# A four-layer transformer kernel: the forget-gate chain in two parts about the compressed keys, compression weights halved between ScalarE and GpSimd, and four other edits in order

## The reference

```python
def hybrid_layer(x, norm_g, w_in, ...):
    h = rmsnorm(x, norm_g)
    proj = h @ w_in
    ...
    o_nsa = nsa_mixer(nsa_q, nsa_kv, nsa_g, cmp_pos, cmp_w1, cmp_b1, cmp_w2, cmp_b2)
    o_pool = pool_mixer(pool_in, pool_w, pool_scale)
    c_x, c_b, c_c = jnp.split(conv_in, 3, axis=-1)
    o_conv = conv_mixer(c_x, c_b, c_c, conv_w)
    f_q, f_k, f_v = jnp.split(fox_qkv, 3, axis=-1)
    o_fox = fox_mixer(f_q, f_k, f_v, fox_f, fox_f_bias)
    ...
def nsa_compress(k, pos_emb, w1, b1, w2, b2):     # the compressed keys and values
    blocks = k[:, idx] + pos_emb                  # 32 tokens each, stride 16
    flat = blocks.reshape(B, nc, NSA_CMP_LEN * hd)
    return jax.nn.silu(flat @ w1 + b1) @ w2 + b2
def fox_mixer(q, k, v, f_logit, f_bias):          # the forget gate
    logf = jax.nn.log_sigmoid(f_logit + f_bias)
    c = jnp.cumsum(logf, axis=1)
    ...
        s = s + jnp.transpose(c_blk, (0, 2, 1))[..., None] - c_keys[:, :, None, :]
def pool_mixer(u, pool_w, pool_scale):            # means over 2, 4, 8, 16 tokens, less u
    ...
    mixed = jnp.einsum('btgc,gcd->btgd', pooled, pool_w).reshape(B, T, C)
    return mixed * pool_scale
```

## Time and profile before

| | |
|---|---|
| median of 3 runs | 2528.85 us (2526.66 to 2528.97) |
| profiled execution, device time | 2527.82 us |
| its span, first to last instruction | 2526.0 us |
| TensorE busy | 2424.8 us (96%) |
| GpSimd busy | 1898.6 us (75%) |
| VectorE busy | 1149.5 us (46%) |
| ScalarE busy | 690.9 us (27%) |
| mean granted TensorE clock | 0.987 |

### The profile page before, as it was taken

One profiled execution on the slowest core, in us unless ns is written; L12 is line 12 of the kernel. 1 busy time (PEld: TensorE's weight loads), 2 busy tenths in 40 slices (PEclk: granted clock), 3 DMA queues, 4 the chain that ended last, 5 costly groups with the idle time before them and its releaser, 6 DMA issues.

```text
span 2526.0 us, 32296 instructions
## 1 busy us (share of the span) xinstructions
PE 2424.8 (96%) x11118; PEld 1871.2 (74%) x11118; DVE 1149.5 (46%) x1587; ACT 690.9 (27%) x1242; POOL 1898.6 (75%) x1553
## 2 busy tenths in 40 slices
PE   7989989999999999899999999999999999999998
PEld 6755768888877843678888777767888877678886
DVE  6576563330261477643322474555322645553323
ACT  2166233330021157233320133144010231450101
POOL 8703578888877753698888799735999998359995
PEclk9999999999999999999999999999999999999999
DMA  4201122222222210122222232201222222112222
GB/s 175 84 9 43 51 75 100 98 93 100 92 75 100 85 41 1 67 100 91 100 97 95 75 113 100 84 34 59 100 97 94 92 100 85 41 53 99 99 99 84
DMA packets 57547, 207.11 MB, mean 82 GB/s; under 512 B 6512, under 2 KB 6896, under 8 KB 57200
## 3 DMA queue, kind: packets, MB, share of 16 engines
q1 hardware_dynamic: 55872, 199.87, 22.2%
q10 hardware_dynamic: 1584, 5.96, 0.6%
HBM read 203.71 MB, written 2.10 MB: 81 GB/s over the span
## 4 chain that ended last, share of the span: by engine, by line
PE 76%; DVE 10%; POOL 7%; issue 4%; ACT 2%; DMA 1%; POOLq 0%; DVEq 0%; ACTq 0%; SPq 0%
PE bank L719 21%; PE bank L721 20%; PE bank L720 20%; POOL w_hi L2526 4%; PE bank L813 4%; PE bank L768 3%; POOL w_lo L2529 3%; PE bank L841 2%; PE bank L867 2%; PE bank L888 1%; DVE branch_lo L1842 1%; DVE moving_lo L1842 1%; DVE x L2168 1%; DVE work L1882 1%; PE bank L906 1%
## 5 line engine op out<-in xcount | busy, mean ns | idle before, releaser
L2526 POOL TENSOR_TENSOR w_hi<-ring,unit 128x512 fp32r<-128x512 f32 x750 | 846.4, 1129 | 497.3 <-PE bank L721 357.0
L2529 POOL TENSOR_TENSOR w_lo<-ring,w_hi 128x512 fp32r<-128x512 f32 x750 | 1010.6, 1347 | 58.7
L719 PE MATMUL bank<-moving_hi,w_hi 128*128 128x512 f32 x1962 | 776.3, 396 | 26.8 <-DVE moving_lo L2137 12.3
L721 PE MATMUL bank<-moving_hi,w_lo 128*128 128x512 f32 x1962 | 768.8, 392 | 0.0
L720 PE MATMUL bank<-moving_lo,w_hi 128*128 128x512 f32 x1962 | 768.7, 392 | 0.0
L719 PEld LDWEIGHTS bank<-moving_hi,w_hi 128*128 128x128 f32 x1962 | 371.5, 189 | 116.9 <-issue 25.7
L720 PEld LDWEIGHTS bank<-moving_lo,w_hi 128*128 128x128 f32 x1962 | 371.4, 189 | 78.8 <-issue 1.9
L721 PEld LDWEIGHTS bank<-moving_hi,w_lo 128*128 128x128 f32 x1962 | 371.1, 189 | 78.4
L2473 DVE TENSOR_TENSOR region<-region,bank 128x512 f32<-128x512 f32 x64 | 39.7, 682 | 278.4 <-PE bank L721 278.4
L719 PE MATMUL bank<-hid_hi,w_hi 128*128 (+1 forms) x352 | 137.7, 391 | 0.0
L1780 ACT ACTIVATE region<-bank 128x512 f32<-128x512 f32 x64 | 38.1, 598 | 363.4 <-PE bank L721 363.4
(11 more groups left out here) (299 smaller groups left out, 3441.1 us busy)
## 6 DMA issues: line engine op xcount, KB each, us to landing
ring<-in_weights SPq DMA_DIRECT2D x375, 512.0 KB, 3.2
x<-in_x_t ACTq DMA_DIRECT2D x4, 512.0 KB, 8.4
out<-region SPq DMA_DIRECT2D x8, 256.0 KB, 2.2
region<-in_tables ACTq DMA_DIRECT2D x1, 1312.0 KB, 9.3
region<-in_tables ACTq DMA_DIRECT2D x1, 1024.0 KB, 5.7
region<-in_p_t ACTq DMA_DIRECT2D x2, 512.0 KB, 4.9
region<-in_tables SPq DMA_DIRECT2D x1, 320.0 KB, 10.4
small_w<-in_small_w ACTq DMA_DIRECT2D x1, 320.0 KB, 5.9
```

The costliest lines, as they stand in the source:

```text
L719: pe.matmul(bank, lhs[0], rhs[0], start=start, stop=False, skip_group_check=True)
L721: return pe.matmul(bank, lhs[1], rhs[0], start=False, stop=stop, skip_group_check=True)
L2526: pool.tensor_tensor(w_parts[0][:, s, at], ring[:, s, at], unit[:, 0:1].broadcast_to([P, BLK // 2]), ALU.mult).then_inc(split_hi, 1)
L2529: pool.tensor_tensor(w_parts[1][:, s, at], ring[:, s, at], w_parts[0][:, s, at].bitcast(F32), ALU.subtract).then_inc(split_ready, 1)
```

## The change

Six edits, none of which changes a result or the number of matmuls:

1. **Start**: ScalarE's four copies of the `vA` banks stand ahead of the sines.
2. **Join**: for the layer norm ahead of a feed-forward, VectorE joins `x = hi + lo` and makes the lower part of `p` behind the feed-forward's loop instead of ahead of it. The residual and ScalarE's scaling of `x` wait for a new semaphore `x_joined`.
3. **Compression weights**: ScalarE makes the upper part of the `w1` blocks (`upper_w1`: two instructions a block, when the block is loaded and the half of the ring is free), at four places of its `project_second`. GpSimd makes the lower part alone and waits for the new semaphore `w1_upper` before it (`split_w1`). These blocks stand outside GpSimd's loops, so its one long loop becomes three.
4. **Forget gate**: the first four instructions of the chain stand ahead of `vc_bd`, the last six behind `cmp_p`.
5. **Pool products**: they are issued in the middle of block conv5 and go to banks 4 to 7. The banks of conv4 and conv5 become 0 and 2.
6. **Heads**: the scores of turn 0 wait for `cb1` and `cu0`, those of turn 1 for `cu1` too, and only the transposes behind them for `pm3`.

```diff
+CONV_BANK = (0, 1, 2, 3, 0, 2)
...
                 for u, i in turns[:AHEAD]:
+                    if second and i == 1:
+                        second()
                     scores(u, i, q, k, extra, causal)
...
+                if opened:
+                    opened()
...
-                for t, before in enumerate(("fv0", "fv1", "fv2", "fv3", "cx0", "cx1")):
+                def pool_products():
+                    prepared_at("pooled")
+                    for g in range(4):
...
+                        pe.matmul(psum[4 + g][rows, :], small_w[rows, at:at + HD], mix[rows, 2 + g // 2, :], start=True,
+                                  stop=True).then_inc(spread, 1)
+
+                for t, before in enumerate(("fv0", "fv1", "fv2", "fv3", "cx0", "cb0")):
                     stored_at(before)
-                    project(("conv", layer, t), psum[t % 4][:], rhs)
+                    project(("conv", layer, t), psum[CONV_BANK[t]][:], rhs, halfway=pool_products if t == 5 else None)
...
-                pe.wait_ge(stored, T["stored"][("pm3", layer)])
+                pe.wait_ge(stored, T["stored"][("cb1", layer)])
+                pe.wait_ge(prepared, T["prepared"][("cu0", layer)])
...
@@ scalar
+                values(range(4), ("vA", 3), lambda i: v_ab[:, i, :], lambda i: psum[i])
+
                 act.wait_ge(setup_dve, SETUP["rest"])
                 act.activation(sin_a, rest[:, 0, :], ACT.Sin)
...
                 raw(("nq1", layer), nq[:, 1, :], psum[1][:], HD ** -0.5)
+                upper_w1(layer, 0)
...
                     store(fqk[:, t, :], psum[2 - 2 * t][:], scale=HD ** -0.5)
+                    upper_w1(layer, 1 + t)
...
                     store(fqk[:, 2 + t, :], psum[1 + t][:])
+                    if t == 0:
+                        upper_w1(layer, 3)
...
+            def upper_w1(layer, i):
+                n = AT[("w1", layer, i)]
+                act.wait_ge(full[n % RING], 16 * (n // RING) + 16)
+                for h, spent in enumerate((half_done, block_done)):
+                    at = slice(h * BLK // 2, (h + 1) * BLK // 2)
+                    act.wait_ge(spent, n - RING + 1)
+                    act.activation(w_parts[0][:, n % RING, at], ring[:, n % RING, at], ACT.Copy).then_inc(w1_upper, 1)
@@ vector
-                dve.wait_ge(parts_ready, T["parts"][("ln", i, KD - 1)])
+                if i % 2:
+                    dve.wait_ge(parts_ready, T["parts"][("ln", i, KD - 1)])
+                    join_parts()
...
-                lower(("p", layer), both(p_parts, np.s_[:, :, :]), p_in_t)
                 with dve.Fori(0, KF // 2) as it:
...
+                join_parts().then_inc(x_joined, 1)
+                lower(("p", layer), both(p_parts, np.s_[:, :, :]), p_in_t)
...
@@ gpsimd
+            def split_w1(n):
+                key, s = BLOCKS[n], n % RING
+                for h in range(2):
+                    at = slice(h * BLK // 2, (h + 1) * BLK // 2)
+                    pool.wait_ge(w1_upper, 8 * key[1] + 2 * key[2] + h + 1)
+                    pool.nop().then_inc(split_hi, 1)
+                    pool.tensor_tensor(w_parts[1][:, s, at], ring[:, s, at], w_parts[0][:, s, at].bitcast(F32),
+                                       ALU.subtract).then_inc(split_ready, 1)
...
+            for layer in range(DEPTH):
+                for i in range(4):
+                    n = AT[("w1", layer, i)]
+                    split_up_to(at, n)
+                    split_w1(n)
+                    at = n + 1
             split_up_to(at, len(BLOCKS))
```

## The result

The changed kernel takes **2499.49 us** (median of 4 runs, 2498.30 to 2500.55), the kernel before beside it 2528.91 (2526.66 to 2530.61). The ratio is 0.9884, 95% interval 0.9872 to 0.9896: 29.4 us saved. The forecast was 2493 and 35.9 us saved. The measured time lies in the range, but at its slower half, so 6.5 us of the forecast gain are missing and have to be found.

What follows compares the result with a forecast made beforehand. TensorE was busy 96% of the span, leaving only its idle time and the pauses' clock cost to gain. Terms 4.3 + 4.8 + 9.8 + 13.0 + 4.0 = 35.9 us gave 2491.9, as a median 2493; range 2486 to 2504.

Steps and rivals of the forecast that it cites:

- Start: Start of the program: ScalarE's copies first let TensorE go on at 35.0 instead of 37.95; 4.3 us with the clock's price.
- Join: Behind the feed-forward loop: the third tile's wait and three short stalls on GpSimd go, 2 x 2.4 us.
- Compression weights: From w1(1) to pool0: ScalarE's upper parts remove TensorE's waits on GpSimd and the clock behind them, 2 x 4.9 us.
- Forget gate: At the transposes of `cmp_p`: the 4.12 us wait and 2.4 us of low clock behind it go, 2 x 6.5 us.
- Pool products: Last convolution matmul to the heads' first maximum: products and stores move into conv5; with the heads, 2 x 2.0 us.
- Heads: Opening of the heads: first maximum 1.2 us after conv5's end, in one term with the pool products, 2 x 2.0 us.
- with slack: At w1(0), where ScalarE comes late: GpSimd ends the block about 0.6 us later than before, with slack.
- The handovers: Rival at the compression weights: handovers between engines eat that gain, 9.8 us go, giving 2503; chance 0.12.
- The new wait in the convolution: Rival: GpSimd late at conv0 to conv2 replaces the wait on `cmp_p`, half of 13 gone, 2499; chance 0.06.
- the borders: Rival at GpSimd's loop entries: four entries each stall for a load's 3.2 us, 13 go, 2506; chance 0.03.
- the first of my marks for "wrong": Sign of a wrong forecast: upper parts by ScalarE that start after GpSimd's previous lower part ended.
- pool0 less than 1 us behind w1(3): Sign of a right forecast, at the end of the compression's weight blocks: pool0 follows w1(3) within 1 us.

## Why the prediction was nearly right, and where not

- **Start** (4.3): 4.22 at the rope. The copies start at 34.36 where I wrote 34.3, `lat` at 35.06 where I wrote 35.0. The 1.14 us that followed were lost in the clock, behind a wait that I had not counted because it did not change. Of the 4.22, 2.89 are the wait (37.95 against 35.06) and 1.33 the clock behind it, where I had 2.95 and, with what I took off, 1.4. That second part rests on one execution. From the first `lat` matmul to the rope it is 36.9 us in the kernel before and 35.6 in the changed one, but the forget gate alone, with the old start and a wait of 3.51 us, has 35.6 too, and the pool products alone, also with the old start, 38.1. At the place where the earlier trace rows show 0.50, the forget gate alone has:

```profile
38.00:40.00 2.00, 1.90 (x8) 1.61 (x9) 1.97 (x3) 1.47 (x4) 1.92 (x2) 1.00 0.70 250
```

  So the 4.22 could have been 2.9 or 5.4 beside another execution of the kernel before: that it came so near to 4.3 is in part luck.
- **Join** (4.8): 5.13 by the trace, 4.8 by the run of it alone, within 2.5 to 7.1. The third tile's wait is gone.
- **Compression weights** (9.8): 5.8. This is the term that was mis-sized, and the failed step is the sentence that w1(0) is made later "with slack". The pair came as worked out, 4.9 + 3.2 = 8.1: in layer 1, GpSimd's fk0 and fk1 splits end 8.09 us apart (2042.02 and 2050.11). But I counted on GpSimd being 2 us ahead, and took 1.0 of that lead away in the same paragraph. Leaving w1(0) to GpSimd brought 3.4 of the missing 4.0 back in the traces, and 1.5 us in device time. The load is the second part: I took the page's 3.2 us from issue to landing, while from the end of a split to GpSimd's next instruction it was 3.3 to 3.5 us in five of these places and 4.7 at fk1 in layer 0. That one load is most of the difference between the layers (3.1 us short in layer 0, 0.9 in layer 1): TensorE's wait behind it was 2.29 us instead of 0.89, and the clock 0.50 at 1551.5 to 1553.5 us, while it stayed at 1.00 in layer 1. What the slow load has and the five others have not is a packet of the queue that brings instructions (view of DMAs, changed kernel, 1542 to 1548 us; packets, MB, share of 16 engines):

```profile
q8 instruction: 1, 0.02, 0.9%
```

  In the five other traces with whole loads and ScalarE's upper parts the same packet meets the same load, which takes 4.1 to 4.2 us from issue to landing. Of all loads of the changed kernel but the first three, 338 have no such packet between issue and landing, and one of them took over 3.6 us; of the 34 that have one, 11 did, up to 5.1. No run moves the packet, so that it is the cause is argued and not shown.
- **Forget gate** (13.0) **and pool products** (4.0): 16.26, alone 12.9 and 4.0 in their stretches. The 0.7 that are missing lie behind pool0 in layer 1 (62.02 against 61.16), where TensorE waits 0.52 us for GpSimd once more, at 2059.52.
- **Heads.** I forecast the first maximum 1.2 us behind the last convolution matmul; it came at 1620.90 - 1619.69 = 1.2. But I stopped there. What also moved is GpSimd's first gate piece: it starts when conv5's last matmul has ended, and that used to be beside the products and is now beside the taps. 2.07 us, half of what the pool products brought; the run of the products alone has the longer first turn too (4.76 against 3.83).
- **Range.** The upper ends of the terms' bounds add up to 4.7 + 5.4 + 11.8 + 13.4 + 4.4 = 39.7 us, which gives 2489 and not the 2486 that I wrote; and their lower ends add up to 13.3 us, which gives 2516 and not 2499. The measured time lies inside either.
- **Rivals.** The handovers did not eat the whole gain of the w1 blocks, but 4.0 of 9.8 went at the first of them and at the loads: this rival (2503) had more truth in it than its 0.12. The new wait in the convolution did not come. GpSimd leaves and enters its loops between fq1, w1(1), fk0 and w1(2) with no idle time but for loads, so the borders cost nothing that shows. No upper part by ScalarE kept GpSimd waiting but that of w1(0), in each layer: the first of my marks for "wrong", met at the one place I had priced at nothing. Of the marks I named, "pool0 less than 1 us behind w1(3)" was met in both layers and said nothing: the time had been lost at fk1 before.

## What to carry to other kernels

A lead of one engine over the next is a stock: write down what every edit adds to it and takes from it, instead of calling a delay "in slack" block by block. In a chain of split and load with two slots, shortening the work alone only uncovers the load; releasing and loading by halves gave more than the edit it was tested against, and nothing without that edit. And when a stretch of one engine is removed, look at what ran beside it on the others: it will now run beside something else.

## What the runs showed of the hardware

- VectorE and GpSimd hold each other up. A tap of 0.48 or 0.75 us took 1.58 and 1.64 beside a lower part and ended 0.3 to 0.6 behind it; a lower part took 1.56 or 1.83 instead of 1.26 where it was the one held; a maximum that reads a bank was not touched. The Trainium skill ("SBUF — State Buffer", SBUF: two separate sides) has it so: an exclusive lock for the whole instruction, taken by GpSimd and by VectorE's fast modes or its instructions with two SBUF inputs. These rows agree that one of the two is held until the other ends, though their starts, 0.04 us apart, do not tell which. The forecast, which set that rule aside for the join, would have done well to ask where else it applies.
- A load of 512 KB takes 3.2 us from issue to landing and one of 256 KB 2.6:

```profile
ring<-in_weights SPq DMA_DIRECT2D x750, 256.0 KB, 2.6
```

  So 0.6 us for 256 KB and 2.0 us that do not depend on the size. The Trainium skill ("SBUF — State Buffer", The DMA setup-cost knee) gives the same 2 us and concludes for DMA-bound transfers that they should be as large as they can be. This kernel's are not of that kind (their packets take 22.7% of 16 engines' span in the page of the changed kernel), and here a smaller transfer did better: 2490.83 us with halves against 2499.49, since the start of the transfer counts here and not its rate.
- The same pause does not always have the same price in clock. 1.33 us of waiting were followed by a clock of 0.51 in one kernel, 1.54 us by 1.00 in another; 2.36 us by 0.51 and by 1.00 in two executions of one kernel; 3.65 us by 0.50 and 3.51 by 1.00 at the old start; 1.33 by 1.00 and 1.32 by 0.50 in the two layers of one execution. A price of the clock that is read from one execution can be another in the next: from the first `lat` matmul to the rope 35.6, 36.9 and 38.1 us with the same code.
